# Scaling the softmax exponentials on ScalarE at the end of its slot list instead of on VectorE

## What is computed

```python
s = jnp.einsum('bqhd,bkhd->bhqk', q_blk, k) * scale
s = s + (F_blk[..., :, None] - Fh[..., None, :])
s = jnp.where(kpos[None, :] <= qpos[:, None], s, NEG_INF)
p = jax.nn.softmax(s, axis=-1)
out = jnp.einsum('bhqk,bkhd->bqhd', p, v)
```

## Time and profile before

| | before |
|---|---|
| time, median of 3 runs | 1364.9 us (1363.17 to 1365.43) |
| time of the profiled execution | 1365.37 us |
| its span, first to last instruction | 1363.6 us |
| PE busy | 1313.4 us, 96% |
| VectorE busy | 737.1 us, 54% |
| ScalarE busy | 355.8 us, 26% |
| GpSimd busy | 608.3 us, 45% |
| mean granted TensorE clock | 0.991 |

### The profile page before, as it was taken

How to read it: one execution, slowest core, us unless ns; L and a number is a source line. 1 busy time by engine, 2 the same in 40 slices (tenths; PEclk the granted TensorE clock), 3 DMA queues, 4 the chain that set the end, 5 groups by cost and what they waited for, 6 DMA issues and landing times. The chain is left out here.

```text
span 1363.6 us, 21210 instructions
## 1 busy us (share of the span) xinstructions
PE 1313.4 (96%) x7595; PEld 1046.9 (77%) x7595; DVE 737.1 (54%) x1077; ACT 355.8 (26%) x525; POOL 608.3 (45%) x287
## 2 busy tenths in 40 slices
PE   8898999999899999999999999999999999999997
PEld 6888888888789986777777777677777776666675
DVE  4757888866666664625557374545534234311327
ACT  3524444443421342111211112021211202111116
POOL 1017686844400238475565766575662112121114
PEclk9999999999999999999999999999999999999998
DMA  7335453511135238777776877778685634477533
GB/s 245 96 120 169 133 189 109 170 59 39 60 119 197 81 118 257 259 241 243 238 253 212 281 252 240 234 238 271 198 283 165 206 127 172 175 270 277 222 138 124
DMA packets 111769, 255.02 MB, mean 187 GB/s; under 512 B 12848, under 2 KB 22961, under 8 KB 106280
## 3 DMA queue, kind: packets, MB, share of 16 engines
q1 hardware_dynamic: 102384, 247.00, 54.5%
q10 hardware_dynamic: 8320, 4.19, 1.1%
q0 software_dynamic: 960, 2.47, 0.5%
HBM read 243.73 MB, written 10.12 MB: 186 GB/s over the span
## 5 line engine op out<-in xcount | busy, mean ns | idle before, releaser
L887 POOL TENSOR_TENSOR WL<-WR,WH 128x1024 fp32r<-128x1024 f32 x55 | 132.9, 2418 | 345.4 <-ACT WH L1120 345.4
L795 POOL TENSOR_TENSOR AR<-AR,QB 128x1024 f32<-128x1024 f32 x96 | 231.9, 2429 | 98.5 <-DMA AR<-cache_k 82.6
L1547 PE MATMUL PSM<-XH,WH 128*128 128x512 f32 x672 | 214.2, 400 | 0.0
L1547 PE MATMUL PSM<-XL,WH 128*128 128x512 f32 x672 | 208.4, 391 | 0.0
L1547 PE MATMUL PSM<-XH,WL 128*128 128x512 f32 x672 | 207.5, 390 | 0.0
L2130 DVE TENSOR_TENSOR ACC<-ACC,PSM 128x512 f32<-128x512 f32 x160 | 108.4, 683 | 141.3 <-PE PSM L1557 141.1
L1547 PEld LDWEIGHTS PSM<-XH,WH 128*128 128x128 f32 x672 | 122.1, 188 | 51.2 <-issue 28.3
L1120 ACT CAST WH<-WR 128x1024 fp32r<-128x1024 f32 x55 | 57.5, 1048 | 364.5 <-PE PSM L1547 186.2
L1557 PE MATMUL PSM<-R 128*128 128x512 f32 x528 | 148.5, 390 | 0.1
L1547 PEld LDWEIGHTS PSM<-XL,WH 128*128 128x128 f32 x672 | 126.4, 188 | 27.7
L1547 PEld LDWEIGHTS PSM<-XH,WL 128*128 128x128 f32 x672 | 126.3, 188 | 27.5
(11 more groups left out here) (275 smaller groups left out, 2174.9 us busy)
## 6 DMA issues: line engine op xcount, KB each, us to landing
AR<-cache_v SPq DMA_DIRECT2D x256, 256.0 KB, 3.4
AR<-cache_k SPq DMA_DIRECT2D x192, 256.0 KB, 3.5
AR<-ws SPq DMA_DIRECT2D x37, 1024.0 KB, 6.4
WR<-ffn SPq DMA_DIRECT2D x66, 512.0 KB, 5.0
WR<-w_in SPq DMA_DIRECT2D x20, 512.0 KB, 4.4
ACC<-cache_k SPq DMA_DIRECT2D x32, 256.0 KB, 2.9
WR<-cache_k SPq DMA_DIRECT2D x32, 256.0 KB, 3.2
WR<-w_o SPq DMA_DIRECT2D x5, 1024.0 KB, 5.1
```

The lines of the kernel that those rows point to most:

```text
L795: pool.tensor_tensor(keys, keys, QB[:].rearrange("p (o n) -> p o n", o=1).to_broadcast([P, KP, AW]), ALU.mult).then_inc(k_mul, 1)
L887: pool.tensor_tensor(lo, WR[:, raw_weight(e), :], hi.bitcast(F32), ALU.subtract).then_inc(ffn_lo, 1)
L1547: ins = pe.matmul(out[:, hc], (hi, lo)[a][:, k * P:(k + 1) * P], x[b][:, k, hc], start=(k == 0 and n == 0), stop=(k == KC - 1 and n == 2))
```

## The change

ScalarE multiplies the exponentials of slot `x` by the reciprocal of the row sum, in an activation with the function Copy and `rinv` as its scale. It stands at the end of ScalarE's list for the slot, behind `entry_hi` and ahead of the first output-projection parts of the last slots, and raises `l_done`. It waits for the reciprocal (`inv_done`), which stays on VectorE. VectorE's multiplication and its wait go.

```diff
                 for n in range(2 * WS, NWT):
                     if ENTRY[n] == x:
                         entry_hi(KC + n)
+                if x < SLOTS:
+                    w = (x % RT + 1) * P
+                    act.wait_ge(inv_done, x + 1)
+                    act.activation(L[x % 2][:, 0:w], L[x % 2][:, 0:w], ACT.Copy, scale=rinv[:, x % 2:x % 2 + 1]
+                                   ).then_inc(l_done, 1)
                 if x == SLOTS - 3:
                     output_hi(0)
...
                     dve.wait_ge(e_done, x + 1)
                     dve.reciprocal(rinv[:, x % 2:x % 2 + 1], rsum[:, x % 2:x % 2 + 1]).then_inc(inv_done, 1)
-                    dve.wait_ge(inv_done, x + 1)
-                    w = (x % RT + 1) * P
-                    dve.tensor_scalar(L[x % 2][:, 0:w], L[x % 2][:, 0:w], rinv[:, x % 2:x % 2 + 1], None, ALU.mult
-                                      ).then_inc(l_done, 1)
```

## The result

The changed kernel takes 1351.6 us (1349.9 to 1355.9, seven runs) against 1363.2 us (1359.4 to 1367.7, seven runs) of the kernel before in the same comparison: a ratio of 0.991, with a 95% interval from 0.9888 to 0.9932, that is 11.6 us less. Of the 6.9 us between 1358.5 and 1351.6, 1.7 us are the base: the median of three runs that the prediction started from was 1364.9 us. The other 5.2 us are the change itself, -11.6 us and not -6.4.

What follows compares the result with a forecast made beforehand. PE, busy 96% of the span, was taken to bound the kernel, with VectorE the crowded engine it waits for in the attention. Seven steps summed to -6.4 us, giving 1358.5 us from the 1364.9 us median; range 1353.5 to 1367.0 us.

Steps and rivals of the forecast that it cites:

- 1, six waits on the scaling: Turnings in the attention: six of PE's seven waits for VectorE's scaling go, -9.0 us, bounds -9.1 and -6.1.
- 2, scores: Attention: PE's two waits for VectorE's next reading of the scores go, -1.6 us, from 0 to -1.6.
- 3, mixer: Mixer's output behind the scalings of slots 61 and 62: half of a 1.2 us wait goes, -0.6 us.
- 4, first slots: First two slots: a copy behind the first scaling on VectorE comes sooner, -0.3 us.
- 5, new waits in 15, 31, 47: Turnings of these slots wait for the scaling at the end of ScalarE's list, +6.2 us, between 5.5 and 6.5.
- 6, slots 9, 25, 41 with L985: New 0.7 us waits per slot, offset by shorter waits for ScalarE's key-row copy: together -0.3 us, +2.1 to -2.4.
- step 7: Last slot: turning waits 0.5 us longer, but VectorE starts L1778 0.75 us sooner; -0.8 us, from 0 to -1.0.
- (a): Rival: PE's waits at the turnings only change the engine charged; -1.6 us, 1363.3 us, no change; chance 0.19.
- (b): Rival: the turning waits for ScalarE in most slots, mean 0.2 us; +6.4 us, 1371.3 us, slower; chance 0.12.
- (c): Rival: Copy needs its own ScalarE table, two loads a slot; at least 51 us more, some 1416 us; chance 0.03.
- (d): Rival: the ends of ScalarE's lists cost nothing in slots 15, 31, 47; -12.6 us, 1352.3 us; chance 0.06.

Runs made afterwards that it cites:

- The narrow kernel before: Kernel before the change, with GpSimd's early key products cut to 64 of 1024 columns each: 1347.4 us, ratio 0.9854.
- The kernel with six slots left on VectorE: Changed kernel, but the scaling stays on VectorE in slots 9, 15, 25, 31, 41 and 47: 1342.8 us, ratio 0.9825 to the kernel before.
- the kernel with narrow products: Changed kernel, with GpSimd's early key products cut to 64 of 1024 columns: 1349.1 us, ratio 0.9886 to the kernel before.

## Why the prediction was wrong, point by point

The gains by slot, changed kernel against kernel before, first profiles, in us:

| step | predicted | measured | where |
|---|---|---|---|
| 1, six waits on the scaling | -9.0 | -11.65 | slots 15 and 16, 31 and 32, 47 and 48: 2.59, 2.56, 2.51; 24 and 25, 40 and 41: 1.79, 1.76; 55: 0.44 |
| 2, scores | -1.6 | -2.65 | slots 21 and 37: 1.33, 1.32 |
| 3, mixer | -0.6 | -1.75 | slots 57 and 63: 0.68, 1.07 |
| 4, first slots | -0.3 | -0.44 | slots 2 and 3; between profiles slot 2 scatters by over 1 us, so that this bears nothing out |
| 5, new waits in 15, 31, 47 | +6.2 | +6.18 | slots 17, 33, 49: 2.14, 2.26, 1.78 |
| 6, slots 9, 25, 41 with L985 | -0.3 | +0.53 | slots 11, 27, 43: 0.70, 0.80, 0.81 later; 12, 28, 44: 0.88, 0.45, 0.45 sooner |
| not in the sum | 0 | -0.63 | slots 19 and 35: 0.31, 0.32 |

With 0.2 us elsewhere this makes -10.6 us between slots 1 and 63 (-9.0 us between the second profiles, the difference in slots 2 and 11). Over the whole span it is -11.0 us in the mean of the profiles, so that what step 7 and all that follows make of it is lost in the scatter.

- **The step that failed: the price of a removed wait, in steps 1 and 2.** The mechanism was right, and all these waits went whole (the upper bound of both). But I put a wait down at the length that the profile shows, 1.99 us for slot 13. The shown gap begins at the modelled end of the last matmul, 133.42 + 0.31 = 133.73 us; without the wait the turning would have started 0.15 us after that matmul's start, as it does in the changed kernel (130.70 and 130.85 us). The wait thus costs 135.72 - 133.57 = 2.15 us, and the steps around it each start some hundredths sooner, and the next slot 0.2 us, once VectorE is not behind. So of the 2.65 us that step 1 measured beyond its -9.0 us, about 1.0 us is this tail of 0.16 us at six waits, 0.9 us are short waits in the slots beside (0.21 us in 16, 32 and 48, 0.15 us in 24 and 40), and the rest are the hundredths. The 0.81 us of a score wait cost 1.33 us in the same way: 0.97 us at the wait itself, 0.24 us at the turning ahead of it, whose short wait stands in no list, and 0.1 us behind it. Even with every step at its best bound the predicted sum is -10.1 us, short of the measured -11.0 us by spans and -11.6 us by times.
- **Step 3, and the 0.63 us not in the sum,** failed for the same reason and one more: I looked for waits in a list that leaves out short ones, so slots 19 and 35 never came up (a shown gap of 0.12 us at the turning ahead of each, which cost 0.28 us); and of the mixer I counted the one wait for L1764 at half (it gave 0.42 us), while two more at the mixer's products, which gave 0.57 and 0.65 us, were not counted. These are rows of the kernel before, of the list of the earlier trace rows; the last is the 0.2 us of the slots 16, 32 and 48 above:

```profile
PE PSM L1364 <- issue: 1.2, 1, 1.2
PE PSM L1364 <- DVE AR L1758: 0.4, 1, 0.4
PE PSM L1353 <- issue: 0.5, 3, 0.2
```

The second is for VectorE's L1758, for the first the profile names no releaser; after the change 0.5 us of these two are left. The narrow kernel before has none of this gain at slots 57 and 63, so it is not GpSimd's early products that were in the way there. The traces show the scalings of slots 51 to 53 and 62 held beside GpSimd's other work, for up to 2.57 us, but no run took that apart.
- **Step 5 was right** to 0.1 us: 2.2, 2.2 and 1.8 us were predicted, the gaps are 2.08, 2.07 and 1.61 us, and with the 0.16 us of a matmul's tail they cost 2.14 to 2.26 and 1.78 us. This step had been worked out from one start time to another (146.49 less 144.25 us), not from a shown gap, so it had the tail in it. The kernel with six slots left on VectorE shows that this price is real.
- **Step 6** was off by 0.8 us: the new waits cost 2.3 us (2.1 predicted), and only 1.8 of 2.4 us came back, since gaps of 0.42, 0.12 and 0.12 us at L985 stayed.
- **Step 7**: the last turning waits 1.72 us, 0.48 more than the earlier trace rows (0.5 predicted), and the remainders' wait behind it went from 2.2 to 1.3 us (0.8 predicted).
- **What it adds:** 49.7 us on ScalarE were predicted, 45.4 came; 72.0 off VectorE, 72.3 went. That the scaling runs beside VectorE's next reading of the scores, at no cost, held too: the next exponential starts within 0.05 us of its extreme in 47 of 64 slots (54 before). In slots 16, 32 and 48 it comes 2.38 us behind it instead of 0.53, but no wait of TensorE names it.
- **The rivals.** (a) fell: the turnings of slots 13, 23, 29, 39 and 45 wait for nothing. (b) fell: ScalarE is waited for in seven slots, not in most. This is where the rule of the Trainium skill pointed (ScalarE: Activation LUTs, Rules for kernel authors: multiply on VectorE). The trace agrees for a scaling that nothing holds, 0.62 us on VectorE against 0.94 us on ScalarE at 768 columns, and not for the 64 as they came, 72.3 us against 45.4 us. That the changed kernel is 5.4 us behind with GpSimd's products narrow speaks neither for the rule nor against it, since it loses that at the ends of ScalarE's lists. (c) fell: 64 more instructions on ScalarE and no load among them. (d) gave nearly the right time (1352.3 us) for a wrong reason: the ends of ScalarE's lists cost 6.2 us, and the removed waits were worth more.
- **The range** was made from doubts about which waits would go. It had no term for a shown wait being worth more than its length, nor for the base, which lay 1.7 us lower, nor for the clock, which moves any single run by steps of 1.7 us.

## What to carry to other kernels

Price a wait of the bounding engine by start times, from the start of the last instruction to that of the waiting one less the usual spacing, and look for late starts that no list of waits names. Before an operation moves to an engine with room as a mean, look at what stands ahead of it in that engine's list in each slot: here 6 of 64 slots gave back 8.5 us of 19.1 (10.6 + 8.5). And where an instruction takes three times its best, find what holds it: that decides between another place, another engine and leaving it in the slots where it is free.

## What the hardware showed beyond that

- VectorE's scaling was held by GpSimd in both forms (2811 ns with a column, where 0.62 us is the unheld time; 2856 ns with two inputs, where it is 0.96 us), the same work on ScalarE never (1163 ns at most in the changed kernel). Not only the products for the samples' keys held it: the same is seen beside GpSimd's remainders and additions (up to 2.57 us).
- The granted clock fell to 1.2 GHz behind a gap of 2.08 us in slot 15 in two of three profiles of one kernel, not behind the equal gap in slot 15 of the kernel with narrow products, and never behind that in slot 31. Low stretches at 10, 540 and 1140 us came and went between profiles. Why one gap is followed by it and another isn't was not settled.
- With lost clock taken off, two executions agree slot by slot within 0.1 us over most of the attention (slots 2 and 11 apart), so a gain of 0.3 us in one slot can be read from single profiles, while the times themselves scatter by several us.
